# First attention: each block of probabilities turned in two 64-query pieces, side by side on the array

## The chip, the cores and the metric

The kernel runs on one core of one Trainium2 chip. The metric is the device time of one execution in microseconds (us); the median of the runs is compared. TensorE (PE) multiplies matrices and loads weights (PEld), VectorE (DVE), ScalarE (ACT) and GpSimd (POOL) do the elementwise work, and SyncE (SP) starts DMAs. Each engine takes its own instructions in order and meets the others at semaphores only.

## The reference

Two transformer layers stand one behind the other, over 512 tokens and 16 meta tokens of width 1024. The first has two feed-forward blocks, and between them a latent attention (MLA) and a gated delta network beside each other. The second has a sliding-window attention and a sparse attention. The change lies in the latent attention of the first layer, whose core is:

```
s = (einsum('bqhd,bkhd->bhqk', qn_b, k_nope) + einsum('bqhd,bkd->bhqk', qr_b, k_rope)) * scale
s = where(k_pos <= q_pos, s, -inf)          # 8 heads, blocks of 128 queries
p = softmax(s, axis=-1)
o = einsum('bhqk,bkhd->bqhd', p, v)
```

## The kernel before, in words

Everything is written out by hand, in raw engine programs: there is no scheduler. The order of the work is the order of the code for each engine, and `wait_ge` and `then_inc` on semaphores tie the engines together.

The latent attention (`latent_attention`, a function of that name for PE, ACT and DVE) works on 16 items, `LATENT`: four blocks of 128 queries, the last block first, times four pairs of heads (heads j and j+4). An item of block g has `4 - g` key tiles of 128 and 16 meta keys, so its rows are 528, 400, 272 or 144 long. It is a pipeline of steps i. In step i PE computes the scores of item i (L923), turns the probabilities of item i-2 so that keys lie on the partitions (L947), and multiplies item i-3 with the values (L973). DVE finds the minima of the scores of item i (L2241 or L2245, then L2234), ACT takes the exponentials of item i (L1581). The turned probabilities of item i-2 lie in PSUM and are copied to SBUF, to the tile PTS1: head j from bank 4 by ACT (L1571), head j+4 from bank 5 by DVE (L2272). In the last item of a block PE also turns the probabilities of the meta keys (PM, L955), multiplies them (L978) and spreads the reciprocal sums (L989).

The semaphores that matter: `exp_rdy` counts exponentials, `pt_ps` counts groups of transposes that are done (two per item), `pt_rdy` and `pc_rdy1` count ACT's and DVE's copies. The transposes of a head wait for its own exponentials and for the copy of its own bank.

Between these steps ACT and DVE do work of the delta network: DVE adds convolution taps (L2042, in `value_taps`), ACT scales first taps (L1600) and takes exponentials (L1611, L1615). Behind the last item ACT takes a tanh over VTANH (L1586), POOL multiplies and adds it (L605, L608), and PE then transposes the values of the delta network (L903).

The second attention, `pair_attention`, much later in the program, turns its probabilities in another way: a 128x128 block is cut in two pieces of 64 queries, which lie on partitions 0 to 63 and 64 to 127. Each piece is a transpose of its own with 64 rows of contraction (L1024), the lower one goes into bank 4 and the upper one into bank 5. The copies (L1631 on ACT, L2345 on DVE) put the pieces together again, with the helper `turned`.

Of the kernel before, what the change touches and what calls it, by code (L numbers as in the profile page):

```python
# [17 lines left out]
P = 128  # L18
D_MODEL, SEQ, N_META, D_FF = 1024, 512, 16, 2816
# [8 lines left out]
CH = 64  # L28
# [49 lines left out]
def build(nc, io):  # L78
    f32, f32r = mybir.dt.float32, mybir.dt.float32r
    ALU, ACT, AX = mybir.AluOpType, mybir.ActivationFunctionType, mybir.AxisListType  # L80
# [138 lines left out]
    PS = ctx.enter_context(nc.psum_tensor("PS", [P, 8, 512], f32))  # L219
# [254 lines left out]

    STEPS = pair_steps()

    def turned(half, i, w):

        src = PS[:, 4 + half, 0:w].rearrange("k (p t q) -> k p t q", p=2, q=CH)
        dst = PTS2[:, i % 2, :, 0:w].rearrange("k p (t c q) -> k p t c q", c=2, q=CH)[:, :, :, half, :]  # L480
        return dst, src
    LATENT = [dict(g=g, qi=QT - 1 - g, j=j, w=P * (QT - g), n=N_META + P * (QT - g), last=j == 3)
              for g in range(QT) for j in range(4)]
# [161 lines left out]
    def _(pe):  # L645
# [261 lines left out]
        def latent_attention():  # L907
            n = len(LATENT)
            for i in range(n + 3):
                if i < n:  # L910
                    x, s = LATENT[i], i % 2
                    if i == WIDE:
                        pe.wait_ge(exp_rdy, 2 * WIDE - 1)
                    elif i > WIDE:
                        pe.wait_ge(exp_rdy, 2 * (i - 1))
                    for p in range(2):
                        h = x["j"] + 4 * p
                        if 0 < i < WIDE:
                            pe.wait_ge(exp_rdy, 2 * (i - 1) + p + 1)
                        q = QH[0:96, h, P * x["qi"]:P * (x["qi"] + 1)]  # L920
                        for k0, k1 in ((0, min(x["n"], SEQ)), (SEQ, x["n"])):
                            if k1 > k0:
                                last = mm(scores(i, p, k0, k1), q, KH[0:96, h, k0:k1], start=True, stop=True)  # L923
                        if i < WIDE or p:
                            last.then_inc(s_ps, 1)
                if i == 0:
                    for t in (3, 4):
                        up_value(t, 3 + t)
                if i == 1:

                    pe.wait_ge(kv_rdy, 8)
                    up_value(0, 4)
                if 2 <= i < 4:
                    per_token(i - 2)
                if i == 2:
                    pe.wait_ge(kn_ps, 9)
                    pe.sem_inc(mm_done, 1)
                if 0 <= i - 2 < n:
                    x, s = LATENT[i - 2], i % 2
                    for p in range(2):  # L940
                        pe.wait_ge(exp_rdy, 2 * (i - 2) + p + 1)
                        if i == 2:
                            pe.wait_ge(kv_rdy, 12)
                        else:
                            pe.wait_ge((pt_rdy, pc_rdy1)[p], i - 2)
                        for t in range(x["qi"] + 1):
                            last = nc.tensor.transpose(PS[:, 4 + p, t * P:(t + 1) * P],  # L947
                                                       PB1[:, s, p, N_META + t * P:N_META + (t + 1) * P], IDENT)
                        last.then_inc(pt_ps, 1)
                        if p == 0 and x["last"]:  # L950

                            pe.wait_ge(gp_ev, 2)
                            if x["g"]:
                                pe.wait_ge(den_rdy, x["g"])
                            nc.tensor.transpose(PS[:, 7, 0:P], PM[:, x["g"] % 2, :, :].rearrange("q h m -> q (h m)"),  # L955
                                                IDENT)
                if i == n + 1:

                    qk_products(0)
                if 0 <= i - 3 < n:  # L960
                    x, s = LATENT[i - 3], (i - 3) % 2
                    pe.wait_ge(pt_rdy, i - 2)
                    pe.wait_ge(pc_rdy1, i - 2)
                    if x["j"] == 0 and x["g"]:
                        pe.wait_ge(o_free, x["g"])
                    if x["j"] == 0:

                        mm(PS[:, 6, :], ZERO[:, :], ZERO[:, :].unsqueeze(1).to_broadcast([P, 4, P]), start=True,
                           stop=False)
                    for t in range(x["qi"] + 1):  # L970
                        for p in range(2):
                            h = x["j"] + 4 * p
                            last = mm(PS[CH * p:CH * (p + 1), 6, P * x["j"]:P * (x["j"] + 1)],  # L973
                                      VM[:, 1 + t, CH * h:CH * (h + 1)], PTS1[:, s, p, t * P:(t + 1) * P],
                                      start=False, stop=False)
                    if x["last"]:
                        for j in range(4):
                            last = mm(PS[:, 6, P * j:P * (j + 1)], VM[:, 0, P * j:P * (j + 1)], PTM[:, :],  # L978
                                      start=False, stop=j == 3)
                    last.then_inc(pv_done, 1)  # L980
                if 0 <= i - 2 < n and LATENT[i - 2]["last"]:

                    g = LATENT[i - 2]["g"]
                    pe.wait_ge(ri_rdy, g + 1)
                    pe.wait_ge(pt_rdy, i - 1)
                    for j in range(4):
                        for p in range(2):
                            f = RI1[:, NH * g + 2 * j + p:NH * g + 2 * j + p + 1].to_broadcast([P, CH])
                            last = mm(PS[CH * p:CH * (p + 1), 7, P * j:P * (j + 1)], f, IDENT, start=True, stop=True)  # L989
                    last.then_inc(den_ps, 1)  # L990
# [226 lines left out]
        for c in range(2):  # L1217
            s = (n + c) % 2
# [146 lines left out]
    def _(act):  # L1365
# [192 lines left out]
        def latent_attention():  # L1558
            n = len(LATENT)
            for i in range(n + 4):  # L1560
# [4 lines left out]
                    A(PM[:, x["g"] % 2, x["j"]:NH:4, :], PB1[:, (i - 1) % 2, :, 0:N_META], ACT.Copy)  # L1565
                if 0 <= i - 2 < n:
                    w, s = LATENT[i - 2]["w"], i % 2
                    act.wait_ge(pt_ps, 2 * (i - 2) + 1)
                    if i >= 4:
                        act.wait_ge(pv_done, i - 3)  # L1570
                    last = A(PTS1[:, s, 0, 0:w], PS[:, 4, 0:w], ACT.Copy)  # L1571
                    act.wait_ge(pt_ps, 2 * (i - 2) + 2)
                    if LATENT[i - 2]["last"]:
                        last = A(PTM[:, :], PS[:, 7, 0:P], ACT.Copy)
                    last.then_inc(pt_rdy, 1)
# [268 lines left out]
    def _(dve):  # L1844
# [378 lines left out]
        def latent_attention():  # L2223
            n = len(LATENT)
            for i in range(n + 6):
# [41 lines left out]
                if 0 <= i - 2 < n:  # L2267
                    w = LATENT[i - 2]["w"]
                    dve.wait_ge(pt_ps, 2 * (i - 2) + 2)
                    if i >= 4:  # L2270
                        dve.wait_ge(pv_done, i - 3)
                    V.tensor_copy(PTS1[:, i % 2, 1, 0:w], PS[:, 5, 0:w]).then_inc(pc_rdy1, 1)  # L2272
                value_taps(i)
                if 0 <= i - 5 < n and LATENT[i - 5]["last"]:
                    qi = LATENT[i - 5]["qi"]
# [610 lines left out]
```

## Time and profile before

| what | us |
|---|---|
| median of 3 runs | 1574.4 (1574.23 to 1575.98) |
| the profiled execution, its own time | 1572.66 |
| its span | 1571.0 |
| PE busy in the span | 1539.7 (98%) |
| PE weight loads busy | 1347.5 (86%) |
| DVE busy | 898.1 (57%) |
| ACT busy | 542.0 (35%) |
| POOL busy | 98.3 (6%) |
| transposes L947, first to last start | 527.1 to 576.5 |

The granted TensorE clock is full in all 40 slices of the page. A row of the timeline gives the start and the length of a group of instructions in us from the span's start, the engine, the line, what is written and read, the shape, and how many there are. For PE the first shape, as 64*128, is the part of the array that is used: rows of contraction by output partitions. A row of the chain gives start, length, engine, what is written and the line, of the work that the end hangs on. Ends of matmuls are modelled.

### The profile page before, as it was taken

What the parts mean: (1) busy time and instruction counts of PE and PEld (TensorE: products, weight loads), DVE (VectorE), ACT (ScalarE), POOL (GpSimd) and SP (SyncE); (2) the same over time, 40 slices, a digit from 0 to 9 for tenths busy, and PEclk for the clock granted to TensorE, in tenths of its full rate; (3) what the DMA queues carried; (4) which work ended last, traced back from release to release, by engine and by line L of the source; (5) the groups of instructions that cost most, each with busy time, mean ns of one, the idle gap of its engine ahead of it and who ended that gap; (6) DMA issues with size and microseconds to landing.
All of it is one profiled execution on the core that took longest, in us unless ns stands there. A gap on an engine that the chain in (4) does not pass through costs nothing.

```text
span 1571.0 us, 30272 instructions
## 1 busy us (share of the span) xinstructions
PE 1539.7 (98%) x12787; PEld 1347.5 (86%) x12787; DVE 898.1 (57%) x1368; ACT 542.0 (35%) x835; POOL 98.3 (6%) x106
## 2 busy tenths in 40 slices
PE   9999999999999999989999999999999999999998
PEld 8999999999998679977888888888888887776777
DVE  6655245565479787555444645533556554457872
ACT  6222122222245573024222333222223143336960
POOL 0000000000001460000000000000000000000410
PEclk9999999999999999999999999999999999999999
DMA  7343333345423200002232222223222253211001
GB/s 285 143 145 108 108 108 140 133 119 131 128 66 103 62 2 31 4 10 74 92 107 97 104 84 103 82 92 108 106 97 75 98 218 134 78 43 55 2 9 74
DMA packets 27668, 147.71 MB, mean 94 GB/s; under 512 B 2928, under 2 KB 3328, under 8 KB 16944
## 3 DMA queue, kind: packets, MB, share of 16 engines
q1 hardware_dynamic: 21616, 122.50, 22.5%
q0 software_dynamic: 5424, 22.68, 5.2%
q8 instruction: 78, 1.28, 0.3%
q10 hardware_dynamic: 528, 1.08, 0.2%
q14 instruction: 22, 0.18, 0.0%
HBM read 140.97 MB, written 5.27 MB: 93 GB/s over the span
## 4 chain that ended last, share of the span: by engine, by line
PE 87%; DVE 7%; ACT 3%; issue 2%; DMA 1%; POOL 1%; SPq 0%; DVEq 0%; ACTq 0%
PE PS L650 24%; PE PS L651 24%; PE PS L652 24%; PE PS L1115 1%; PE PS L1100 1%; PE PS L1050 1%; PE PS L1010 1%; PE PS L1113 1%; ACT PB L1650 1%; PE PS L923 1%; PE PS L1024 1%; DMA SILUC<-in_c 1%; DVE WLO L1855 1%; PE PS L1328 1%; DMA H<-in_h 1%
## 5 line engine op out<-in xcount | busy, mean ns | idle before, releaser
L650 PE MATMUL PS<-UH,WHI 128*128 128x264 f32 (+1 forms) x1088 | 326.7, 300 | 3.0 <-DVE WLO L1855 3.0
L651 PE MATMUL PS<-UH,WLO 128*128 128x264 f32 (+1 forms) x1088 | 325.3, 299 | 0.0
L652 PE MATMUL PS<-UL,WHI 128*128 128x264 f32 (+1 forms) x1088 | 325.0, 299 | 0.0
L1375 ACT ACTIVATE WHI<-RAW 128x2048 fp32r<-128x2048 f32 (+3 forms) x124 | 210.3, 1696 | 310.7 <-PE PS L652 304.3
L1855 DVE TENSOR_TENSOR WLO<-RAW,WHI 128x2048 fp32r<-128x2048 f32 (+3 forms) x124 | 251.1, 2025 | 76.9 <-ACT WHI L1375 76.3
L650 PEld LDWEIGHTS PS<-UH,WHI 128*128 128x128 f32 x1088 | 204.7, 188 | 10.1 <-DVE WLO L1855 2.6
L651 PEld LDWEIGHTS PS<-UH,WLO 128*128 128x128 f32 x1088 | 204.6, 188 | 6.5 <-issue 0.2
L652 PEld LDWEIGHTS PS<-UL,WHI 128*128 128x128 f32 x1088 | 204.3, 188 | 6.2
L650 PE MATMUL PS<-UHS,WHI 128*128 128x512 f32 x520 | 205.4, 395 | 0.0
L652 PE MATMUL PS<-ULS,WHI 128*128 128x512 f32 x520 | 202.5, 389 | 0.0
L651 PE MATMUL PS<-UHS,WLO 128*128 128x512 f32 x520 | 202.4, 389 | 0.0
L1429 ACT ACTIVATE TANH<-SILU 128x528 f32<-128x528 f32 (+1 forms) x44 | 28.1, 639 | 257.1 <-DVE SILU L1919 257.0
L650 PEld LDWEIGHTS PS<-UHS,WHI 128*128 128x128 f32 x520 | 97.6, 188 | 22.3 <-issue 2.2
L651 PEld LDWEIGHTS PS<-UHS,WLO 128*128 128x128 f32 x520 | 97.6, 188 | 20.8 <-issue 1.0
L652 PEld LDWEIGHTS PS<-ULS,WHI 128*128 128x128 f32 x520 | 97.6, 188 | 20.3
L651 PE MATMUL PS<-GH,WLO 128*128 128x264 f32 x352 | 100.5, 285 | 0.0
L652 PE MATMUL PS<-GL,WHI 128*128 128x264 f32 x352 | 100.2, 285 | 0.0
L650 PE MATMUL PS<-GH,WHI 128*128 128x264 f32 x352 | 99.6, 283 | 0.0
L1919 DVE TENSOR_TENSOR SILU<-PS,RSTD 128x528 f32<-128x528 f32 (+1 forms) x44 | 30.8, 699 | 103.2 <-PE PS L652 103.2
L1944 DVE SCALAR_TENSOR_TENSOR H<-PS,H 128x528 f32<-128x528 f32 (+3 forms) x32 | 22.3, 698 | 112.6 <-PE PS L652 112.6
L650 PE MATMUL PS<-GHS,WHI 128*128 128x512 f32 x176 | 68.6, 390 | 0.0
L651 PE MATMUL PS<-GHS,WLO 128*128 128x512 f32 x176 | 68.5, 389 | 0.0
(429 smaller groups left out, 2679.6 us busy)
## 6 DMA issues: line engine op xcount, KB each, us to landing
RAW<-in_f2u SPq DMA_DIRECT2D x22, 1024.0 KB, 4.8
RAW<-in_f1u SPq DMA_DIRECT2D x21, 1024.0 KB, 4.8
ADA<-in_ada POOLq DMA_DIRECT2D x24, 512.0 KB, 4.8
RAW<-in_f1d SPq DMA_DIRECT2D x16, 704.0 KB, 4.0
RAW<-in_f2d SPq DMA_DIRECT2D x16, 704.0 KB, 4.1
RAW<-in_wi SPq DMA_DIRECT2D x10, 1024.0 KB, 4.8
RAW<-in_w SPq DMA_DIRECT2D x8, 1024.0 KB, 4.8
RAW<-in_mg SPq DMA_DIRECT2D x8, 1024.0 KB, 4.8
```

The source lines that it names most:

```text
L650: mm(out, WHI[:, slot, c:c + w], hi, start=first, stop=False)
L651: mm(out, WLO[:, slot, c:c + w], hi, start=False, stop=False)
L652: return mm(out, WHI[:, slot, c:c + w], lo, start=False, stop=last)
L923: last = mm(scores(i, p, k0, k1), q, KH[0:96, h, k0:k1], start=True, stop=True)
L1010: last = mm(PS[:, 2 - 2 * s + p, o:o + m], P2[rows, q, P * x["qi"]:P * (x["qi"] + 1)], P2[rows, 10 + x["b"], a:a + m], start=True, stop=True)
L1024: last = nc.tensor.transpose(PS[:, 4 + c, o:o + CH], PB2[rows, s, p, t * P:(t + 1) * P], IDENT[rows, rows])
L1050: last = mm(PS[rows, 6, P * y["j"]:P * (y["j"] + 1)], v, PTS2[:, s, p, o:o + P], start=t == 0, stop=t == tiles_ - 1)
L1375: A(WHI[:, slot, 0:w], RAW[:, slot, 0:w], ACT.Copy).then_inc(hi_rdy, 1)
L1429: A(TANH[:, slot, 0:w], SILU[:, slot, 0:w], ACT.Tanh, scale=0.5).then_inc(tanh_rdy, 1)
L1855: TT(WLO[:, slot, 0:w], RAW[:, slot, 0:w], WHI[:, slot, 0:w].bitcast(f32), ALU.subtract).then_inc(lo_rdy, 1)
L1919: TT(SILU[:, slot, 0:w], psum(4 * slot, w), RSTD[:, c0:c0 + w], ALU.mult).then_inc(gn_rdy, 1)
L1944: STT(h, psum(4 * slot, w), 0.25, h, ALU.mult, ALU.add)\
```

## The change

The latent attention turns its probabilities the way the second attention does. Each 128x128 transpose becomes two with 64 rows of contraction each, one for each half of the queries; the lower half goes to bank 4 and the upper half to bank 5, for both heads. So each bank now holds a half of both heads. The waits follow from this. No transpose of an item starts before both copies of the item before are done (`pt_rdy` and `pc_rdy1`). `pt_ps` is raised only when all transposes of the item are done, by both halves, and so ACT's copy waits for all of them, as DVE's did before. The transpose of the meta keys stands ahead of the item's other transposes and no longer between the two heads. The copies write PTS1 through `turned`, in pieces of 64 elements.

```diff
-    def turned(half, i, w):
+    def turned(half, i, w, probs=PTS2):
...
-        dst = PTS2[:, i % 2, :, 0:w].rearrange("k p (t c q) -> k p t c q", c=2, q=CH)[:, :, :, half, :]
+        dst = probs[:, i % 2, :, 0:w].rearrange("k p (t c q) -> k p t c q", c=2, q=CH)[:, :, :, half, :]
...
                 if 0 <= i - 2 < n:
                     x, s = LATENT[i - 2], i % 2
+                    if i == 2:
+                        pe.wait_ge(kv_rdy, 12)
+                    else:
+                        pe.wait_ge(pt_rdy, i - 2)
+                        pe.wait_ge(pc_rdy1, i - 2)
+                    if x["last"]:
+
+                        pe.wait_ge(exp_rdy, 2 * (i - 2) + 2)
+                        pe.wait_ge(gp_ev, 2)
+                        if x["g"]:
+                            pe.wait_ge(den_rdy, x["g"])
+                        nc.tensor.transpose(PS[:, 7, 0:P], PM[:, x["g"] % 2, :, :].rearrange("q h m -> q (h m)"), IDENT)
                     for p in range(2):
                         pe.wait_ge(exp_rdy, 2 * (i - 2) + p + 1)
-                        if i == 2:
-                            pe.wait_ge(kv_rdy, 12)
-                        else:
-                            pe.wait_ge((pt_rdy, pc_rdy1)[p], i - 2)
                         for t in range(x["qi"] + 1):
-                            last = nc.tensor.transpose(PS[:, 4 + p, t * P:(t + 1) * P],
-                                                       PB1[:, s, p, N_META + t * P:N_META + (t + 1) * P], IDENT)
-                        last.then_inc(pt_ps, 1)
...
+                            for c in range(2):
+                                rows, o = slice(CH * c, CH * (c + 1)), (p * (x["qi"] + 1) + t) * CH
+                                last = nc.tensor.transpose(PS[:, 4 + c, o:o + CH],
+                                                           PB1[rows, s, p, N_META + t * P:N_META + (t + 1) * P],
+                                                           IDENT[rows, rows])
+                                if p == 1 and t == x["qi"]:
+                                    last.then_inc(pt_ps, 1)
...
-                    act.wait_ge(pt_ps, 2 * (i - 2) + 1)
+                    act.wait_ge(pt_ps, 2 * (i - 2) + 2)
...
-                    last = A(PTS1[:, s, 0, 0:w], PS[:, 4, 0:w], ACT.Copy)
-                    act.wait_ge(pt_ps, 2 * (i - 2) + 2)
+                    last = A(*turned(0, i, w, PTS1), ACT.Copy)
...
-                    V.tensor_copy(PTS1[:, i % 2, 1, 0:w], PS[:, 5, 0:w]).then_inc(pc_rdy1, 1)
+                    V.tensor_copy(*turned(1, i, w, PTS1)).then_inc(pc_rdy1, 1)
```

On PE, in steps 4 to 6 of the latent attention, this stands in the order before; L923 are the scores, L947 and L955 the transposes, L973, L978 and L989 the products:

```order
L923 MATMUL PS<-KH,QH 128x400 x2
L947 MATMUL PS<-TAB,PB_94 128x128 x8
L973 MATMUL PS<-PTS_95,VM 64x128 x8
L923 MATMUL PS<-KH,QH 128x400 x2
L947 MATMUL PS<-TAB,PB_94 128x128 x4
L955 MATMUL PS<-TAB,PM 128x128
L947 MATMUL PS<-TAB,PB_94 128x128 x4
L973 MATMUL PS<-PTS_95,VM 64x128 x8
L989 MATMUL PS<-TAB,RI_103 64x128 x8
```

And this after the change, where the lines have other numbers (L957 for L947, L951 for L955, L978 for L973, L994 for L989):

```order
L923 MATMUL PS<-KH,QH 128x400 x2
L957 MATMUL PS<-TAB,PB_94 128x64 x16
L978 MATMUL PS<-PTS_95,VM 64x128 x8
L923 MATMUL PS<-KH,QH 128x400 x2
L951 MATMUL PS<-TAB,PM 128x128
L957 MATMUL PS<-TAB,PB_94 128x64 x16
L978 MATMUL PS<-PTS_95,VM 64x128 x8
L994 MATMUL PS<-TAB,RI_103 64x128 x8
```

Eight transposes of 128 columns became sixteen of 64 columns, and that of the meta keys moved from the middle to the front. At the end of the stage, in the last step that turns anything, PE has this order before (L887 and L888 begin the products of the delta network):

```order
L947 MATMUL PS<-TAB,PB_94 128x128
L955 MATMUL PS<-TAB,PM 128x128
L947 MATMUL PS<-TAB,PB_94 128x128
L887 MATMUL PS<-PRC 64x64
L888 MATMUL PS<-PRC 64x64
```

and this after, with its waits:

```order
L951 MATMUL PS<-TAB,PM 128x128 [waits per_token_read,exp_ready,factors_t_ready,pair_probs_copied_1,probs_t_ready]
L957 MATMUL PS<-TAB,PB_94 128x64 [waits exp_ready]
L957 MATMUL PS<-TAB,PB_94 128x64
L957 MATMUL PS<-TAB,PB_94 128x64 [waits exp_ready]
L957 MATMUL PS<-TAB,PB_94 128x64
L887 MATMUL PS<-PRC 64x64
```

Here the meta keys' transpose and all four others stand ahead of ACT's copy of the item, where one transpose stood ahead of it before.

## Rows read from the trace of the kernel before

**Rows 1.** Windows: us; busy time (count) of PE, PEld, DVE, ACT, POOL; clock; DMA; GB/s

```profile
532.00:549.00 17.00, 17.00 (x148) 12.86 (x147) 9.77 (x32) 10.90 (x32) 14.13 (x15) 1.00 0.05 9
549.00:575.00 26.00, 23.68 (x207) 17.52 (x206) 24.83 (x73) 19.76 (x72) 17.74 (x16) 1.00 0.01 1
```

**Rows 2.** Chain of the latent attention, where it runs on PE and leaves it

```profile
532.47 1.02 PE PS L947 x8
...
546.93 1.36 PE PS L923 x4
548.31 0.73 DVE NMF L2245
```

**Rows 3.** Timeline: start, length, engine, line; scores, transposes, products in steps 3 to 6

```profile
532.40 1.09 PE L947 MATMUL PS<-TAB,PB 128*128 128x128 f32 x8
...
533.25 0.48 PE L968 MATMUL PS<-ZERO 128*128 128x512 f32 x1
...
534.69 1.61 PE L923 MATMUL PS<-KH,QH 96*128 96x400 f32 x4
...
535.80 0.14 PEld L947 LDWEIGHTS PS<-TAB,PB 128*128 128x128 f32 x1
...
536.13 1.04 PE L947 MATMUL PS<-TAB,PB 128*128 128x128 f32 x8
...
537.10 1.09 PE L973 MATMUL PS<-PTS,VM 128*64 128x128 f32 x16
...
544.00 0.82 PE L947 MATMUL PS<-TAB,PB 128*128 128x128 f32 x6
...
544.75 1.09 PE L973 MATMUL PS<-PTS,VM 128*64 128x128 f32 x16
```

**Rows 4.** Timeline of the second attention: its half-height transposes and what follows

```profile
1482.52 0.59 PE L1024 MATMUL PS<-TAB,PB 64*128 64x64 f32 x12 [0.57 <-issue]
1483.04 0.88 PE L1050 MATMUL PS<-PTS,VT 128*64 128x128 f32 x12
...
1508.93 0.71 PE L1024 MATMUL PS<-TAB,PB 64*128 64x64 f32 x16 [0.23 <-issue]
1509.57 1.09 PE L1050 MATMUL PS<-PTS,VT 128*64 128x128 f32 x16
```

**Rows 5.** Timeline: from a 128*128 transpose to a 64*64 product

```profile
576.51 0.29 PE L947 MATMUL PS<-TAB,PB 128*128 128x128 f32 x1
...
576.73 0.33 PE L887 MATMUL PS<-PRC 64*64 64x64 f32 x2
```

**Rows 6.** Timeline: the copies of turned probabilities in both attentions

```profile
528.26 0.69 DVE L2272 COPY PTS<-PS 128x512 f32<-128x512 f32 x1 [0.55 <-PE PS L947]
...
533.10 0.60 ACT L1571 ACTIVATE PTS<-PS 128x512 f32<-128x512 f32 x1 [3.05 <-PE PS L947]
...
1508.16 0.68 DVE L2345 COPY PTS<-PS 128x512 f32<-128x512 f32 x1
...
1509.68 0.60 ACT L1631 ACTIVATE PTS<-PS 128x512 f32<-128x512 f32 x1 [0.77 <-PE PS L1024]
```

**Rows 7.** Timeline: steps 9 and 11, a late copy and the scores DVE takes

```profile
553.50 0.51 DVE L2272 COPY PTS<-PS 128x384 f32<-128x384 f32 x1
...
554.16 0.52 PE L947 MATMUL PS<-TAB,PB 128*128 128x128 f32 x3
...
560.07 1.08 PE L923 MATMUL PS<-KH,QH 96*128 96x272 f32 x4
...
561.58 0.46 DVE L2245 TENSOR_REDUCE NMF<-PS 128x2 f32<-128x288 f32 x1 [0.15 <-DVE OTF L2286]
```

**Rows 8.** Chain at the end of the stage

```profile
576.25 0.32 PE PS L947
576.59 0.27 ACT PTS L1571
...
577.01 1.96 ACT VTANH L1586
...
589.69 1.61 PE PS L903 x48
```

More of the change, by code:

```diff
@@ L939, in latent_attention @@
                     x, s = LATENT[i - 2], i % 2
+                    if i == 2:
[9 more added lines that the diff above has]
+                        nc.tensor.transpose(PS[:, 7, 0:P], PM[:, x["g"] % 2, :, :].rearrange("q h m -> q (h m)"), IDENT)
                     for p in range(2):
                         pe.wait_ge(exp_rdy, 2 * (i - 2) + p + 1)
-                        if i == 2:
-                            pe.wait_ge(kv_rdy, 12)
-                        else:
-                            pe.wait_ge((pt_rdy, pc_rdy1)[p], i - 2)
                         for t in range(x["qi"] + 1):
-                            last = nc.tensor.transpose(PS[:, 4 + p, t * P:(t + 1) * P],
-                                                       PB1[:, s, p, N_META + t * P:N_META + (t + 1) * P], IDENT)
-                        last.then_inc(pt_ps, 1)
[L950 to L956, printed above, removed]
+                            for c in range(2):
[5 more added lines that the diff above has]
+                                    last.then_inc(pt_ps, 1)
                 if i == n + 1:
```

## The prediction

> **What bounds the kernel now.** I read the page first: PE is busy nearly all the time, at the full clock. So I asked whether PE is also what the latent attention waits for, and took the busy time by stretches [rows 1]. From 532 to 549 us PE is busy for 17.00 of 17.00 us and DVE for 9.77: the stretch is PE's. From 549 to 575 DVE is busy for 24.83 of 26.00 us: that stretch is DVE's. The chain of waits says the same and gives the border. It runs over PE's transposes (532.47) and on to the scores of step 7 (546.93), and there it goes over to DVE's minimum at 548.31 [rows 2]. DVE holds it until the last exponentials. At the end it is one string: a transpose, ACT's copy, the tanh over VTANH at 577.01, work on POOL, and PE's transposes of the values at 589.69 [rows 8]. So time saved on PE up to the scores of step 7 brings DVE's stretch forward. After that a faster transpose is worth nothing, and only the last step, on the closing string, counts again.
>
> **How PE's rows join.** Two facts are needed for every step. First, a matmul starts 0.17 us before the modelled end of the one before where both use the whole array: the scores end at 534.69 + 1.61 = 536.30 and the transposes start at 536.13. Where the array is cut in another way, it starts only 0.07 before: the transposes end at 537.17, the products on 128*64 start at 537.10 [rows 3]. A 128*128 transpose that ends at 576.80 is followed by a 64*64 product at 576.73, again 0.07 [rows 5]. So a change of cut costs 0.10 us. The reader is to see that the change adds one such change of cut per item, between the scores (96*128, the whole array) and the new transposes (64*128). From the transposes to the products there was one already.
> The Trainium skill says it in "TensorEngine Tiling (Array Packing)", section Tiling Modes: changing the tiling mode, not just the tile, drains the engine. The trace agrees, with 0.10 us as the price here. By the same page's table of speedups, up to two times and no drain counted, the sum below would be larger; that is my third rival, worked out there from rows alone.
>
> **The price of the transposes.** Four key tiles, before: from the scores' end to the products' start 537.10 - 536.30 = 0.80 us [rows 3]. After: the rows of the second attention have exactly the new form, 64*128 with 64x64, and from the first of sixteen to the products it takes 1509.57 - 1508.93 = 0.64 [rows 4]. With the start 0.07 ahead of the scores' end that is 0.57. Saved: 0.23 us.
> Three key tiles, before: the scores of step 6 have the same length and join (544.00 + 0.17 = 544.17), and the products start at 544.75: 0.58. After: 1483.04 - 1482.52 = 0.52, less 0.07, is 0.45. Saved: 0.13.
> One pitch of the small transposes, by the row of sixteen, is (0.71 - 0.22)/15 = 0.033 us, with 0.22 as the part of a single one; of the large ones (1.04 - 0.27)/7 = 0.11. That is 0.066 for a pair of pieces against 0.11.
>
> **Along the chain.**
> - Step 2: the scores of item 3 wait for an exponential that stands behind ACT's copy. The copy came 533.10 - 532.40 = 0.70 us after the first transpose [rows 3, 6], with half of them done. It now needs all sixteen: 1509.68 - 1508.93 = 0.75 [rows 4, 6]. Cost 0.05.
> - Step 3: from the first transpose to the zero product it takes 533.25 - 532.40 = 0.85, and 0.64 after: saved 0.21. The next scores also wait for an exponential behind the copy, so no more than about 0.2 can be had. I take 0.21.
> - Steps 4 and 5: 0.23 each. Step 5 has the meta transpose too, which is only moved; I take it at the same.
> - Step 6: 0.13.
> - Saved up to DVE's start at 548.31: 0.21 + 0.46 + 0.13 - 0.05 = 0.75 us.
>
> **DVE's stretch.** It is passed on whole if nothing in it gets later. The copies cost the same with pieces of 64: 0.68 and 0.69 on DVE, 0.60 and 0.60 on ACT [rows 6]. The added wait (both copies before any transpose) bites where DVE's copy is late. In step 9 that copy ends at 554.01 and the second head's transposes start at 554.16, while the first head's had started earlier; now all start there. Queued behind them on PE are the products and the scores of the next steps. The cost is up to two large groups' worth, 0.2 to 0.3 us, and DVE asks for those scores late: the tightest I found are the scores of step 11, modelled end 561.15, taken at 561.58 [rows 7]. That is 0.43 of room, so I count nothing. If that room were gone, it would cost 0.1 to 0.2 in each of two or three steps.
>
> **The closing string.** Before, one transpose stands ahead of ACT's copy: 576.59 - 576.25 = 0.34 [rows 8]. After, the meta transpose stands first (a pitch of 0.11), then a change of cut (0.10), then four small ones, 3 x 0.033 + 0.22, then the 0.03 to ACT's start that the sixteen show: 1509.68 against 1509.64. In all about 0.55: cost 0.21. The meta keys' copy follows ACT's copy at once, and the tanh follows that. POOL and then PE at 589.69 follow without another entry, so the shift goes through, and the rest of the kernel is PE's.
>
> **Sum.** -0.75 + 0.21 = -0.54 us. The profiled execution took 1572.66 us (span 1571.0 and 1.66 around it), so it would take 1572.1. The median of the runs shown lies 1.7 above that execution, at 1574.4; less 0.54 it is 1573.9. A difference of 0.2%, 3.1 us, is about what a measurement of this kernel can tell from none, so this forecast is "no change".
>
> **Rivals.**
> 1. The gain never leaves the stage: DVE's stretch is held by something that does not move, such as POOL, which is busy for 14.13 of 17.00 us in PE's stretch and for 17.74 of 26.00 in DVE's [rows 1] and feeds exponentials on ACT. Then only the closing 0.21 is left: 1574.6. Against it: the chain shows no POOL between 532 and 577. Chance 0.12.
> 2. Slower. The change of cut from 96*128 to 64*128 is in no row, and it may undo the early weight load: the load of the first large transpose starts 536.13 - 535.80 = 0.33 us ahead of it [rows 3]. If that is the price and not 0.10, steps 4 and 5 save nothing, step 6 costs 0.10, and the closing string costs 0.44. With steps 2 and 3 as above the sum is 0.05 - 0.21 + 0.10 + 0.44 = +0.38: 1574.8. The same mechanism decides for slower from a price of 0.23 on, since four places on the chain have it and there is 0.54 to lose. With the room of step 11 gone as well, it is +0.8: 1575.2. For it: nothing but the missing row. Against it: every join of two cuts that I found shows 0.07. Chance 0.15.
> 3. A larger gain: the change of cut hides behind the scores. Then 0.33 is saved in steps 4 and 5, 0.23 in step 6, 0.21 in step 3, and 0.05 and 0.11 are lost: -0.94, 1573.5. Chance 0.13.
> 4. The pieces do not run side by side here. A piece then takes half of 0.11, the sixteen as long as the eight did, and with the change of cut each item costs 0.10 more: 0.05 + 0.4 + 0.21 is +0.7, 1575.1. Rows 4 show the same form with the same tiles at 0.033. Chance 0.03.
> My forecast has 0.57.
>
> All of these lie within 0.2% of 1574.4. What is left for a real change is something outside my sums: the shift of the later stages against their DMAs, or a median on another level, as the 1575.98 among the runs shows. I give faster by over 0.2% 0.04, slower by over 0.2% 0.04, and within 0.92. The range takes in the rivals from 1573.5 to 1575.2, and on both sides the scatter of the runs: 1572.4 to 1575.6.
>
> **What the profile after would show.** Right: transposes of 64*128 in groups of sixteen lasting about 0.7; from the scores' end to the products 0.57 instead of 0.80; DVE's minimum of step 7 about 0.75 us earlier, 547.6; the tanh at about 576.5; PE's transposes of the values at about 589.2; copies of unchanged length; busy time of the transposes' stretch on PE smaller, with gaps where DVE's stretch is. Wrong: a gap of more than 0.2 us between the scores and the transposes (rival 2), a group of sixteen that lasts about 1.0 (rival 4), or DVE waiting for scores between 549 and 575 where it did not before.

## The result: slower, by TensorE's clock

The median of 22 runs is 1584.75 us (1574.05 to 1604.23), of the kernel before, beside them, 1574.26 us (1572.60 to 1576.22). The ratio is 1.0052 [1.0036, 1.0068]. It leaves out the four executions that lie more than 1.5% above the kernel's fastest, so here the spread says more: eleven of the 22 runs took 1574 to 1582 us, seven 1587 to 1594, four 1599 to 1604. The kernel before was run 132 times in all beside the kernels of this study, and never took more than 1577.5.

The profiled execution of the changed kernel is one of the short ones, 1575.92 us with a span of 1574.2. Where the forecast looked, it came out nearly as worked out. The timeline of PE (start, length, engine, line), against [rows 3]:

```profile
536.20 1.61 PE L923 MATMUL PS<-KH,QH 96*128 96x400 f32 x4
537.75 0.71 PE L957 MATMUL PS<-TAB,PB 64*128 64x64 f32 x16
538.39 1.09 PE L978 MATMUL PS<-PTS,VM 128*64 128x128 f32 x16
...
543.78 1.61 PE L923 MATMUL PS<-KH,QH 96*128 96x400 f32 x4
545.32 0.58 PE L957 MATMUL PS<-TAB,PB 64*128 64x64 f32 x12
545.84 1.09 PE L978 MATMUL PS<-PTS,VM 128*64 128x128 f32 x16
```

The scores end at 537.81 and the products start 0.58 us later, where 0.57 was forecast; with three key tiles it is 0.45, as forecast. The windows that answer to [rows 1], shifted by the 1.61 us that this execution is late by then:

```profile
533.61:550.61 17.00, 17.00 (x190) 11.87 (x192) 10.32 (x35) 10.85 (x32) 14.06 (x15) 1.00 0.04 8
550.61:576.61 26.00, 23.34 (x238) 17.32 (x234) 24.86 (x71) 20.00 (x71) 18.31 (x16) 0.93 0.01 2
```

PE and DVE are as busy as before, but the column behind the counts, the granted clock, is 0.93 in the second window where it was 1.00. The same view around the places where it falls:

```profile
484.00:489.00 5.00, 5.00 (x30) 5.00 (x31) 4.87 (x9) 0.35 (x1) 0.00 (x0) 0.66 0.31 108
566.00:571.00 5.00, 3.48 (x33) 2.91 (x33) 4.93 (x13) 2.88 (x12) 3.48 (x3) 0.66 0.00 2
577.00:582.00 5.00, 4.39 (x79) 3.98 (x80) 0.98 (x2) 3.26 (x7) 1.07 (x1) 0.66 0.00 0
1444.00:1452.00 8.00, 7.32 (x68) 5.65 (x65) 5.08 (x20) 6.52 (x29) 1.26 (x1) 0.57 0.01 2
```

A mean of 0.66 over 5 us is 3.4 us at half the clock (1.2 GHz instead of 2.4). The trace of the kernel before has such a stretch only at its very end. But that trace is one of its best: of its 110 executions beside the experiments below 20 have a mean clock of 1.000, the others 0.995 to 0.999, so short falls of the clock belong to the kernel before too. The short executions of the changed kernel have 0.990 to 0.998, the others 0.977 to 0.988. The third of the rows is why [rows 8] came out late: the last meta transpose, its four companions and ACT's copy fall into it.

```profile
577.61 0.48 PE L951 MATMUL PS<-TAB,PM 128*128 128x128 f32 x1 [0.91 <-ACT PTS L1576]
578.01 0.47 PE L957 MATMUL PS<-TAB,PB 64*128 64x64 f32 x4
```

```profile
578.56 0.28 ACT L1576 ACTIVATE PTS<-PS 128x128 f32<-128x128 f32 x1 [0.59 <-PE PS L957]
578.73 0.27 ACT L1578 ACTIVATE PTM<-PS 128x128 f32<-128x128 f32 x1
578.89 1.97 ACT L1590 ACTIVATE VTANH<-PRC 128x2112 f32<-128x2112 f32 x1
```

From the first transpose to ACT's copy it takes 0.95 us here; in an execution with the full clock there (e13 below) 577.13 - 576.46 = 0.67, against 0.34 before and 0.55 forecast.

### The profile page after: what moved, and what is told of

Read it like the earlier page. It is cut to its first block, busy times and chain, and to the rows that moved or that the text cites. A ratio compares the mean times of both kernels' runs of the same rounds, so it can differ in the third digit from the quotient of the medians.

```text
span 1574.2 us, 30405 instructions
## 1 busy us (share of the span) xinstructions
PE 1543.8 (98%) x12867; PEld 1350.7 (86%) x12867; DVE 897.3 (57%) x1368; ACT 542.4 (34%) x835; POOL 98.7 (6%) x106
## 4 chain that ended last, share of the span: by engine, by line
PE 89%; DVE 5%; ACT 2%; issue 1%; DMA 1%; POOL 1%; SPq 0%; DVEq 0%; ACTq 0%
PE PS L650 24%; PE PS L651 24%; PE PS L652 24%; PE PS L1015 1%; PE PS L1055 1%; PE PS L1120 1%; PE PS L1105 1%; PE PS L923 1%; PE PS L1118 1%; PE PS L1029 1%; ACT PB L1654 1%; DMA SILUC<-in_c 1%; PE PS L1333 1%; DMA H<-in_h 1%; DVE WLO L1859 1%
```

## Experiments

I use three terms. A **short stretch** is up to 14 us at 1.2 GHz, in the traces at 484, between 530 and 587, at 679 or between 1442 and 1457. A **long stretch** is 17 to 51 us at 1.2 GHz in the delta network's products on 64x64 parts of the array, behind 607 us. **Number** is the count of all of TensorE's instructions in the trace (weight loads, matmuls, and those on semaphores and registers) from its start, modulo 256.

**e1: again, for a profile of a long run.** No edit.

> The changed kernel once more, for the spread of its runs, each with its granted clock. Theory A (clock): all of the excess over 1574 us comes from stretches in which TensorE is granted 1.2 GHz, so the runs spread over 1574 to 1604 us again, and the time rises by about the missing clock share times the span (a mean clock of 0.985 goes with about 1590, 0.995 with about 1576). Theory B (chip or day): the 22 runs met a disturbance, and now the runs lie at 1573 to 1576 with a mean clock of 1.00. Theory C (my sum wrong in the latent attention, no clock in it): the runs lie together at one time, about 1575 to 1576.

1590.66 us (1576.86 to 1604.20), ratio 1.0091 [1.0055, 1.0126]. The profiled run took 1591.34. Its windows; what matters is the first number, PE busy (count), and the clock:

```profile
621.00:624.00 3.00, 3.00 (x111) 3.00 (x108) 2.32 (x9) 0.00 (x0) 0.00 (x0) 1.00 0.98 319
624.20:627.50 3.30, 2.72 (x94) 2.61 (x91) 1.48 (x5) 0.00 (x0) 0.00 (x0) 1.00 0.04 12
627.58:651.47 23.89, 23.89 (x455) 23.89 (x452) 7.46 (x20) 0.40 (x1) 0.00 (x0) 0.50 0.01 3
```

For 23.89 us PE is busy all the time at half the clock and does 455 matmuls; at the rate of the first row (111 in 3 us) they take 12.3. So 11.6 us are lost here. What comes before, by the timelines of SP and of PE:

```profile
620.07 0.38 SPq L518 DMA_DIRECT2D RAW<-in_mg  x1
```

```profile
624.40 0.30 PE L1120 MATMUL PS<-TTT,AB 64*64 64x32 f32 x4
625.28 0.31 PE L1118 MATMUL PS<-AB,TTT 64*64 64x32 f32 x4 [0.58 <-issue]
...
627.52 0.41 PE L1120 MATMUL PS<-TTT,AB 64*64 64x32 f32 x4
627.69 0.45 PE L1118 MATMUL PS<-AB,TTT 64*64 64x32 f32 x4
```

PE stands still for 0.58 us and waits for no semaphore ("issue"). From 627.69 on a group of four takes 0.45 us instead of 0.30. The stop comes behind the 1 MB load of the mg weights. The queue that carries instructions (q8 of the page, here 16 KB for every 256 instructions of TensorE) has a packet at 617.50 and the next only at 623.01, 1.9 us into the load; with the full clock they otherwise come every 3.6 us or so. That gave the theory: a fetch is held up behind the load, TensorE runs out of instructions, and the pause takes its clock down.

**e2: the new waits without the pieces** (128x128 transposes, both copies awaited, the meta transpose ahead).

```diff
-                            for c in range(2):
-                                ...
+                            last = nc.tensor.transpose(PS[:, 4 + p, t * P:(t + 1) * P],
+                                PB1[:, s, p, N_META + t * P:N_META + (t + 1) * P], IDENT)
```

> Before's 128x128 transposes in before's layout, with the new waits alone: both copies before any transpose, ScalarE's copy behind all transposes, the meta keys' transpose first. If the longer waits of TensorE lower its clock, this kernel spreads as the changed one does: median 1580 or more, mean clocks down to 0.98. If the form of the transposes does it (half the columns, two pieces at once, so less work in the same time), it stays within 1573 to 1577 with a clock of 0.998 or more.

1574.76 us (1573.21 to 1580.47), ratio 1.0011 [1.0000, 1.0022]. That is neither of the two outcomes expected. Seven of 12 runs are below 1575 and five at 1578.4 to 1580.5: the waits alone bring short stretches (one of 6.8 us at 533.4 in the profile), but no long one.

**e3 and e4: the new form in the first eight items, or in the last eight.**

```diff
+    def CUT(k):
+        return k < 8        # e4: k >= 8
```

> The new form for items 0 to 7 (four and three key tiles, mostly the stretch that TensorE bounds), before's form and waits for items 8 to 15. If the clock falls because TensorE has too little to do at the end of the stage (items 8 to 15, which VectorE bounds), this kernel keeps the clock: 1573.0 to 1576, median about 1573.7. If the denser first half matters (its scores and products come sooner and so leave gaps later), the spread stays: median 1580 or more.

> The complement: before's form for items 0 to 7, the new form and waits for items 8 to 15. If too little work at the end of the stage lowers the clock, this spreads as the changed kernel does: median 1580 or more, mean clocks down to 0.98. If the first half is the cause, it stays at 1574 to 1577.

e3: 1590.26 us, ratio 1.0118 [1.0091, 1.0145]; all six runs at 1586.7 to 1600.6. e4: 1580.78, ratio 1.0049 [1.0027, 1.0071]; four of nine runs above 1585. Neither half is innocent, and the first half, where the gain was, is the worst of all. It stops at 621.43 us for 0.93 us, and a stretch of 27.3 us follows. It adds 105 instructions to TensorE's stream, e4 adds 39, the whole change 145 (160 more weight loads and matmuls, 15 fewer on semaphores).

**e5 and e6: only the number of instructions.** Tiny transposes into unused places, in step 2 and in the last step: 72 in the kernel before (144 instructions with their weight loads), 56 in the changed one (112 more, 257 in all).

```diff
+        def pads(bank, times):
+            for _ in range(times):
+                nc.tensor.transpose(PS[0:32, bank, 0:CH], IDENT[0:CH, 0:32], IDENT[0:CH, 0:CH])
```

> Before, word for word in its transposes and waits, with 72 tiny transposes (32x64, into banks that are free, read by nobody) on TensorE: 36 in step 2, where it waits for an exponential, and 36 in the last step, where it waits for a copy. They make 144 more instructions; the change made 145 more. Theory F (fetch): the change moves the points at which TensorE's instructions are fetched, in pieces of 16 KB, so that one falls due while the 1 MB load RAW<-in_mg runs, about 1 us behind its start; TensorE runs dry for 0.6 to 0.9 us in the solve of the delta network, and the clock stays at 1.2 GHz for 24 to 27 us. Then this kernel, with nothing of the change in it, has runs at 1586 to 1591 too, in a third of them or more. Theory W (waits and form of the transposes): no such run, all within 1572.5 to 1577.

> The changed kernel with 56 such tiny transposes, 28 in step 2 and 28 in the last step: with the 145 of the change that is 257 more instructions than before, and a fetch of 16 KB is 256 instructions, so the fetches behind the latent attention come due where they did before. Theory F: no run at 1586 or above; what is left are the short stretches at 1.2 GHz, 1573.5 to 1581. Theory W: the spread stays, with runs at 1588 to 1604.

e5: 1583.45 us, ratio 1.0071 [1.0038, 1.0104], six of 12 runs at 1588.0 to 1599.4. With 144 instructions that do nothing the kernel before spreads as the changed one does. e6: 1575.58, ratio 1.0006 [0.9997, 1.0015], one of 12 runs high (1598.92). The changed kernel loses them, but for one, with 112 more. e6 alone doesn't tell the count from the place of the pads: 28 of them also stand in PE's pause ahead of step 3, which e12 below shows to matter. e5 has pads in the same pause, and its high runs all the same.

**e7: 257 more as well, and PE's pauses filled** by twelve matmuls of 128x384.

```diff
+                    count = {9: 1, 11: 1, 12: 1, 13: 3, 15: 1, 16: 1, 17: 2}.get(i, 0)
+                        fills(7, count)
```

> The changed kernel with fillers in the latent attention, full products of 128x384 into banks that are free: two in step 2 and ten over steps 9 to 17, ahead of the waits for the copies, and 32 tiny transposes, so that the instructions again come to 257 more than before. If the short stretches at 1.2 GHz in the latent attention come from the waits of TensorE, they go: the clock is at 0.997 or above in all runs, as before, and the time is 1572.5 to 1576. If the form of the transposes or anything else lowers the clock, stretches between 530 and 590 us remain, and runs at 1577 to 1581.

1576.83 us, ratio 1.0015 [1.0006, 1.0023], all 11 runs at 1576.1 to 1578.5, clock 0.998 to 1.000. The clock came out as expected, the time above the 1572.5 to 1576. Without short stretches the runs lie close together, but the fillers cost 2 us, because they stand on the chain.

**e8: the load 2 us later** in the changed kernel.

```diff
+            if name == "mg":
+                sp.wait_ge(a_ps, 10)
```

> The changed kernel, with one wait more: SyncE issues the loads of the mg weights only after the tenth product of the delta network is there, about 2 us later than now, so that the instruction fetch that falls due about 1 us behind the first of them goes out ahead of it. TensorE's instructions are the changed kernel's, one for one. Theory (the fetch is held up behind the 1 MB load, TensorE runs dry for 0.6 to 0.9 us, and its clock then stays at 1.2 GHz for 24 to 27 us): no run at 1586 us or above, all between 1573.5 and 1581, the median 1576 to 1578, what is left above the kernel before being the short low stretches in the latent attention. Rival (the turning in pieces keeps the clock down by itself, wherever the fetch falls): runs stay spread from 1575 to 1604 as in the changed kernel, half of them above 1586. Second rival (any wait of SyncE there delays the weights): all runs slower by the length of a wait for the weights of the delta network that shows on TensorE.

1585.92 us (1583.23 to 1591.55, five runs), ratio 1.0075 [1.0062, 1.0088]. The expectation failed, but not the theory, which I had applied wrongly: the fetch after the one I spared is now held up. It goes out at 630.12, number 202, in the load's last 0.4 us, and the stretch of 17.1 us begins at 634.65.

**e9: a version meant to be good**: the first eight items in the new form, one filler in the pause ahead of step 3, the load later.

```diff
+    def CUT(k):
+        return k < 8
...
+                if i == 2:
+                    fills(6, 1)
```

> The new form for the first eight items of the latent attention (where the copies are short), the old form for the other eight (where VectorE's longer copies gave time back), one matmul of 128x384 in the pause of TensorE ahead of the third step, whose result is not used, and the load of the mg weights 2 us later. Theory: no run at 1586 us or above, median 1573.4 to 1574.4, 0 to 0.5 us below the kernel before: 0.5 us gained by the first scores-limited steps, less some 0.2 for the matmul added. Rival (the gain of the first eight items is swallowed whole by VectorE and GpSimd behind it): 1574.5 to 1575. Rival of the clock by itself: spread as in the changed kernel.

1573.99 us against 1574.37, ratio 1.0001 [0.9993, 1.0010]: no loss, and no gain that can be told. One of 12 executions took 8305 us at the full clock; its cause is open.

**e10 and e11: the load made small, or cut in four** in the changed kernel.

```diff
+                if isinstance(n, int) and n == START["mg"]:
+                    sp.dma_start(RAW[:, slot, 0:CH], src[:, 0:CH]).then_inc(raw_ld[slot], 16)
+                    return
```

```diff
+                    for c in range(3):
+                        sp.dma_start(RAW[:, slot, c * w // 4:(c + 1) * w // 4],
+                                     src[:, c * w // 4:(c + 1) * w // 4]).then_inc(row_st, 16)
+                        sp.wait_ge(row_st, 32 + 16 * (c + 1))
+                    sp.dma_start(RAW[:, slot, 3 * w // 4:w], src[:, 3 * w // 4:w]).then_inc(raw_ld[slot], 16)
```

> The changed kernel, but the first load of the mg weights brings 64 columns in place of 2048 (the rest of that slot keeps older weights, so the merge works with other numbers). Every wait and every instruction of TensorE is the changed kernel's. Theory (a fetch of 256 of TensorE's instructions that falls due about 1 us behind the 1 MB load is held up until the load has passed, at an instruction number above 200 of its 256, TensorE runs dry, and the clock stays low in the 64x64 products behind it): with next to nothing loaded there, no fetch between 612 and 640 us comes later than 120 of its 256, no low stretch begins between 620 and 640 us in the profile, and no run is at 1586 us or above; median 1575.5 to 1578.5, the short low stretches in the latent attention being left. Rival (TensorE's work itself, or where the clock stands when the delta network begins, sets the long stretch): half the runs stay above 1586 us, up to 1604.

> The changed kernel, but the first load of the mg weights goes in four parts of 256 KB, each issued by SyncE when the one before has landed (8 us in all instead of 4.8, with 80 us until anyone needs it). Theory: a fetch then waits for 256 KB at most, about 0.7 us, and TensorE does not run dry: no run at 1586 us or above, median 1575.5 to 1578.5. Rival (any traffic of this load holds the fetch up, whatever its size), and rival of TensorE's work itself: runs above 1586 us stay, half of them.

e10: 1579.07 us, ratio 1.0024 [1.0015, 1.0034]. The band of 1587 to 1594 is gone, but one of ten runs took 1600.83, where none above 1586 was expected. e11: 1579.91, ratio 1.0029 [1.0010, 1.0048], five of 13 runs above 1585: the expectation failed. Its profiled run (1602.28) corrected the theory:

```profile
604.00:607.00 3.00, 3.00 (x110) 3.00 (x108) 3.00 (x8) 2.37 (x7) 0.00 (x0) 1.00 0.03 5
607.50:610.50 3.00, 2.91 (x85) 2.65 (x86) 2.93 (x8) 3.00 (x4) 0.00 (x0) 1.00 0.03 8
610.61:661.81 51.20, 51.20 (x966) 51.20 (x964) 18.57 (x45) 4.04 (x7) 0.00 (x0) 0.50 0.09 23
```

The clock falls at 610.61, where the network begins and 15 us ahead of the load. PE was idle for 0.09 us of the 3 before; it did 85 matmuls where it did 110 just ahead. So there is a second starting point, the entry into the network, and it costs most: 966 matmuls in 51.20 us, some 25 us lost. The thinner work there is not enough to bring the fall: e1 passes the same place in the same way, and its clock stays full:

```profile
607.50:610.50 3.00, 2.91 (x88) 2.55 (x84) 2.93 (x8) 3.00 (x3) 0.00 (x0) 1.00 0.03 8
```

Both kinds end only where the 64x32 products give way to others. The lines of PE in e11 from 655 to 664 us, around the stretch's end at 661.81:

```profile
L1138 PE MATMUL PS<-VB,TTT 64*64 64x64 f32 x58 | 4.5, 252 | 0.0
L1140 PE MATMUL PS<-TTT,KBG 64*64 64x64 f32 x56 | 4.2, 248 | 0.0
L1127 PE MATMUL PS<-TTT,AB 64*64 64x32 f32 x72 | 4.1, 291 | 0.0
```

The clock comes back within the wide products (64x64) of L1138 and L1140, and in e1, e3, e8, e12 and e15 within the same two lines. So in these traces the narrow products run at the full clock where they begin with it, and in none of the six did it come back before the wide ones. Why was not tested.

**e12 and e13: one filler in the pause ahead of step 3; and with it the small load** of e10.

```diff
+                if i == 2:
+                    fills(6, 1)
```

> The changed kernel with one matmul of 128x384 more (its result isn't used), ahead of the turning of the first item, in the pause of TensorE before the third step. Theory of two starting points: the stretch at 532 us goes (3 to 5 us of it per run that had one), the runs at 1598 to 1604, which begin at the entry into the network after that stretch, go or get rare, but those at 1586 to 1594, from the load, stay in a quarter or a third of the runs; median 1576 to 1580. If the 532 stretch is behind both: no run at 1586 or above. If the load alone is behind both: half the runs stay at 1586 or above, up to 1604.

> The same filler, and the first load of the mg weights brings 64 columns in place of 2048 (the merge works with older weights in the rest of that slot). Theory of two starting points: neither is left, no run at 1586 us or above, all between 1573.5 and 1580, median 1575 to 1577. If a third cause exists, runs at 1586 or above stay.

e12: 1578.36 us, ratio 1.0025 [1.0006, 1.0044]; three of 12 runs at 1588.7, 1591.0 and 1597.8, as expected. Its profiled run has no stretch at 532, but stops behind the load:

```profile
622.59 0.24 PE L1156 MATMUL PS<-TTT,AB 64*64 64x32 f32 x1 [1.22 <-issue]
```

e13: 1574.95 us, ratio 1.0004 [0.9995, 1.0013], all 11 runs at 1572.6 to 1576.3. Filler and small load together leave no time above 1576.3, as expected. The stretch at 530 to 534 hangs on the pause ahead of step 3: six of the eight traces with a pause of 1.37 to 1.40 us have it, none of the nine with less or with pads or fillers in its place. The rows in the kernel before, in the changed one and in e12:

```profile
529.15 2.34 PE L923 MATMUL PS<-KH,QH 96*128 96x512 f32 x8 [0.93 <-ACT PB L1581]
```

```profile
530.84 2.33 PE L923 MATMUL PS<-KH,QH 96*128 96x512 f32 x8 [1.40 <-ACT PB L1585]
```

```profile
531.33 0.70 PE L940 MATMUL PS<-KH,QH 96*128 96x512 f32 x1 [0.56 <-ACT PB L1622]
```

A pause does not decide by itself. One of 1.94 to 2.00 us stands ahead of 484 us in all 17 traces, long before the change; nine have a stretch of 3.4 us behind it, eight have none, the kernel before among them:

```profile
483.76 0.39 PE L650 MATMUL PS<-UH,WHI 128*128 128x264 f32 x1 [1.98 <-DVE WLO L1855]
```

**The fetch and the load in 14 traces.** Counted from the records: number when the load's first packet moves, number when the held fetch goes out, and the stop.

| trace | at the load | at the fetch | PE's stop, us |
|---|---|---|---|
| before | 181 | 157 | none |
| e2 | 168 | 154 | none |
| e6, e7 | 186, 184 | 146, 144 | none |
| e14 | 183 | 161 | none |
| e9, e4 | 200, 223 | 170, 176 | none |
| after, e5 | 70, 70 | 72, 66 (0.0 us from the load's start, in time) | none |
| e8 | 236 | 202 | 0.49 |
| e1 | 70 | 204 | 0.58 |
| e3, e12 | 30, 76 | 234, 234 | 0.93, 1.22 |
| e15 | 72 | 253 | 1.48 |

All five stops come at number 49 exactly, four behind instruction 11825 and e8's behind 12081, which is 256 later. The later the fetch, the longer the stop. In all twelve traces in which the fetch is held, with a stop or without, the instruction of the next number 49 starts 2.2 to 2.5 us after the fetch goes out, never sooner. A fetch with a number up to 176 leaves at least that much work, one from 202 on does not. "None" means no idle row: between two starts at number 49 there are up to 0.31 us (the kernel before, e4), where 0.03 is usual, so these two are close to a stop. And the first column can be worked out: 181 + 145 = 326, which is 70 modulo 256; 181 + 105 gives 30; 181 + 39 gives 220; 181 + 257 gives 182. At 70 a fetch falls due just as the load starts, so chance decides which goes first. At 30 all six runs were high. e4, at 223, had four of nine runs high, and none of those was profiled: the table doesn't explain them.

The Trainium skill ("Runtime: NRT & Kernel Launch", section Instruction fetch mechanics) has the blocks of 256 instructions and a fetch queue of the sequencer's own, and says that the cost is mostly hidden. The trace agrees in size, with a fetch every 3.6 us, and disagrees on the cost: 0.49 to 1.48 us of standstill in five traces.

**e14 and e15: GpSimd's addition out of VectorE's way** (the kernel before, the changed one).

```diff
-            G2(units(IX, b), units(IX, b), over(tab("mlater", 0, CH), UB), ALU.add).then_inc(px_d, 1)
+            G1(units(IX, b), units(IX, b), 0.0, None, ALU.mult).then_inc(px_d, 1)
```

> The kernel before, but GpSimd multiplies its block of index scores by zero (a TENSOR_SCALAR) in place of adding the mask of later tokens (the TENSOR_TENSOR of L602): values differ, order and waits don't. Theory (a convolution tap of VectorE takes 0.76 us alone and up to 1.50 beside GpSimd's TENSOR_TENSOR, not beside its TENSOR_SCALAR): the twelve taps take under 11.0 us in sum against 11.95, and the scores-start to the tanh string 52.0 to 52.9 us against 53.28. Rival (the taps' length has another cause, as their tiles): 11.9 us as before.

> The same edit in the changed kernel. Theory: the taps take the same sum as in the kernel before with that edit, within 0.2 us (12.64 against 11.95 now), and what the scores gained by VectorE's seventh step (0.52 us) reaches the tanh string to 0.3 us or more, unless the clock is low in between. Rival: the taps stay some 0.7 us longer than in the kernel before with that edit, and the gain is given back as now.

One execution each: 1572.98 and 1588.19 us, the second with a stop and a stretch of 30.7 us. In both the clock is full from 525 us until a short stretch at 575.9 and 576.1. DVE's eight taps into TAB (groups by line: busy us, mean ns), in the kernel before, the changed one, e14 and e15, in this order:

```profile
L2042 DVE SCALAR_TENSOR_TENSOR TAB<-PRC,COL,TAB 128x528 f32<-128x528 f32 x8 | 8.3, 1075 | 0.0
```

```profile
L2046 DVE SCALAR_TENSOR_TENSOR TAB<-PRC,COL,TAB 128x528 f32<-128x528 f32 x8 | 9.3, 1199 | 0.0
```

```profile
L2042 DVE SCALAR_TENSOR_TENSOR TAB<-PRC,COL,TAB 128x528 f32<-128x528 f32 x8 | 7.1, 927 | 0.0
```

```profile
L2046 DVE SCALAR_TENSOR_TENSOR TAB<-PRC,COL,TAB 128x528 f32<-128x528 f32 x8 | 7.2, 934 | 0.0
```

A tap takes 0.76 us alone and 0.88 to 1.51 beside a TENSOR_TENSOR of GpSimd. All twelve take 11.96 us before, 12.63 after, 10.78 in e14 and 10.51 in e15. From the scores of item 2 to the tanh it is 53.28, 53.54, 53.25 and 51.87 us. e14 missed the 52.0 to 52.9 expected: it gained 0.35 us from DVE's minimum of step 7 to that of step 15, and lost 0.33 behind it, in the short stretch, which the kernel before has not. Between e14 and e15, which both have it, the change gains 1.38 us, more than was expected: 0.52 up to step 7, 0.62 in DVE's stretch, 0.25 behind. The taps differ by 0.27 us where 0.2 was expected at most. So the theory for DVE holds, on one execution of each.

## Why the prediction was wrong, step by step

- **What bounds the kernel now** read the clock as a fixed property of the kernel: the page showed it full in every slice. It is not fixed, not even in the kernel before. This is the step that failed: the sum put the clock, and what 145 more instructions do to the fetches behind them, at nothing, and the runs showed 11.6 us lost in one long stretch (e1) and some 25 in another (e11). "Something outside my sums" got 0.04 for slower, and it was the result. "The shift of the later stages against their DMAs" stood there as an example, without a mechanism or a price; it is what happened, with the instruction fetch as what shifts.
- **The price of the transposes** held to 0.01 us (0.58 and 0.45 measured), the change of cut with it. Rivals 2, 3 and 4 fall by the same rows.
- **Along the chain**: -0.52 us up to DVE's step 7, where -0.75 was forecast. Taken between starts of scores, step 2 costs 0.08 (0.05), step 3 gains 0.17 (0.21), step 4 0.23 (0.23), step 5 only 0.05 (0.23), step 6 0.14 (0.13). Step 5 has the meta transpose, now ahead of the others; I had taken it as merely moved.
- **DVE's stretch** was to pass the gain on whole. It gave back 0.42 us from step 7 to step 15: DVE runs earlier against GpSimd, and more of its taps meet the additions of L596 and L602 (taps +0.67 us). e14 and e15 bear this out, each with one execution: without the additions of L602 the stretch passes the gain on. The room of 0.43 us at the scores of step 11 went too: their modelled end is 562.08 and DVE takes them at 562.12, after 0.22 us of waiting for PE, a sign that the forecast had named as wrong. In e15 DVE waits there for 0.21 as well and the gain still comes through, so it cost little. Rival 1 had the outcome (gain lost before the tanh) and GpSimd's name, but as something that holds DVE by a wait, not as a neighbour that lengthens its instructions.
- **The added wait** was counted as nothing because no chain runs over it. Its pauses did not lengthen the chain; in some executions they came with a fall of the clock (e2, the waits alone: five of 12 runs at a mean clock of 0.995 or 0.996; e7, pauses filled: none under 0.998). The pause of step 13 grew from 0.77 us to 1.68, and the clock fell within it; e13 has the same pause, and there it did not fall:

```profile
567.52 0.45 PE L951 MATMUL PS<-TAB,PM 128*128 128x128 f32 x1 [1.68 <-ACT PTS L1576]
```

- **The closing string**: to the tanh 577.46 - 576.46 = 1.00 us at the full clock (e13), 0.76 before: +0.24, forecast +0.21.
- **Sum**: at the full clock it is -0.51 + 0.45 + 0.14 = +0.08 us in e13 (scores of item 2 to DVE's step 7, from there to step 15, and on to the tanh), and -0.07 in e9, where half the items are in the old form. Forecast was -0.54. The half microsecond that failed here is no part of the 10 us that the median lost: the eleven short runs have their middle at 1577.9, 3.6 above the kernel before, with more of the short stretches than it has, and the eleven others lie 14 to 30 above it. Of those the seven up to 1594 fit a stop behind the load (e1's trace), and the four from 1599 on a fall at the entry (e11's); no execution of the 22 above 1576 was profiled.

Shown: instructions that do nothing bring times above 1586 us to the kernel before (e5); the fetch is late in every trace with a stop, and the stop's end follows it by 2.2 to 2.5 us; the stop moves with the load (e8); with the load and the pause gone no such time is left in 11 runs (e13). Fitting, but not separated from the pads' place: that 112 more take them away (e6). Open: what decides at the entry into the network. The clock stayed up through the same entry in the other 16 traces. e13 shows only that with the load and the pause gone it did not happen in 11 runs. The profile doesn't show either what keeps the kernel before from it. Open too are e4's four high runs. And the changed kernel itself stood in two of the six sets of runs only, so the spread of the variants is compared across sets; the kernel before, in all six, kept its median at 1574.2 to 1574.5.

## What to carry to other kernels

A change that adds TensorE instructions shifts every later instruction fetch against every DMA. Where a large load starts shortly ahead of the point at which a fetch falls due (here 1.5 us or less), the engine can run dry, and in narrow products (64x32 here) the clock then stayed down until wider ones came. So compare not only medians but the spread of runs and the clock of each, look at idle rows marked "issue", and try a hundred idle instructions more before blaming or praising an edit. A wait that is off the chain need not be free on TensorE: behind pauses of 1.4 us ahead of step 3 the clock fell in six of eight traces.

## What the runs showed of the hardware

- 16 KB of instructions go to TensorE every 256 instructions, and the page counts them (q8) on the same 16 DMA engines as data. Behind a 1 MB load such a fetch went out 1.9 to 3.5 us after the load's first packet, and up to 6.1 us after the fetch before it (613.95 to 620.09, e3). TensorE stood still for up to 1.48 us, and the first instruction that hung on the fetch started 2.2 to 2.5 us after it went out.
- The clock fell to 1.2 GHz with PE busy for 97% of the time before it (e11: 2.91 of 3.00 us), and stayed there for 51.20 us with PE busy for 51.20. The Trainium skill ("TensorE: Matmul & The Clock Gate", section HAM oscillation — how this bites in real kernels) tells of a clock that falls in waits between bursts of matmuls. The short stretches that follow pauses agree (1.4 us ahead of step 3, 1.94 to 2.00 ahead of 484), though the same pauses left the clock full in other traces; e11's long stretch has only 0.09 us of waiting in the 3 us before it.
- A DVE SCALAR_TENSOR_TENSOR of 128x528 takes 0.76 us alone, 0.76 to 1.09 beside GpSimd's TENSOR_SCALAR and 0.88 to 1.51 beside its TENSOR_TENSOR of 128x384. The Trainium skill ("SBUF — State Buffer", section Who interferes with whom) says that the two share one pair of ports, which one holds alone. The trace agrees that they disturb each other; that it depends on the kind of GpSimd's operation stands only in the runs.
